# A two-block model layer on one core: index dots between the parts of the value products, gate weights split ahead of Silu, the output product's last chunks by row tile, squares by halves

## The reference

```
h = rmsnorm_2(x, norm_g[l]);  proj = h @ w_in[l]
q, k, v, ga, iq, ik, iw, xr, gr, ma, mb = split(proj)      # rope on q, k, iq, ik
dots  = einsum('bqhd,bsd->bqhs', iq, ik)                   # 16 index heads of 64
score = einsum('bqh,bqhs->bqs', iw, relu(dots));  sel = top_k(score, 64)
attn  = attention over the selected keys                   # 8 heads of 128
y_a = (attn * silu(ga)) @ w_out_attn[l]
hr  = rg_lru(causal_depthwise_conv(xr));  y_b = (hr * silu(gr)) @ w_out_rnn[l]
x = x + (sigmoid(ma) * y_a + sigmoid(mb) * y_b) @ w_o[l]
```

## Time and profile before

| | us |
|---|---|
| median of 3 runs | 1961.88 |
| lowest and highest run | 1961.56, 1962.95 |
| profiled execution, its own time | 1964.03 |
| its span, first to last instruction | 1962.3 |
| second block, first transposes to the end | 1190.3 to 1962.3 |

### The profile page before, as it was taken

How to read it: one execution, slowest core, us unless ns; L and a number is a source line. 1 busy time by engine, 2 the same in 40 slices (tenths; PEclk the granted TensorE clock), 3 DMA queues, 4 the chain that set the end, 5 groups by cost and what they waited for, 6 DMA issues and landing times.

```text
span 1962.3 us, 28235 instructions
## 1 busy us (share of the span) xinstructions
PE 1865.8 (95%) x11294; PEld 1267.1 (65%) x11294; DVE 835.5 (43%) x1885; ACT 671.0 (34%) x1277; POOL 268.9 (14%) x239
## 2 busy tenths in 40 slices
PE   8999999999998999999999999999999999999997
PEld 7784444434447774444444446878889868798996
DVE  4763212211215762111211215556665654756665
ACT  4532111111114531111111113456555444574653
POOL 1400000000000400000000004771000067600000
PEclk9999999999999999999999999999999999999999
DMA  8468999999995469999999995452335744442353
GB/s 290 176 267 372 417 428 426 429 429 428 428 420 193 179 272 389 414 427 427 429 429 429 428 419 201 150 191 87 127 102 180 258 150 161 169 146 89 122 175 114
DMA packets 121431, 557.58 MB, mean 284 GB/s; under 512 B 5009, under 2 KB 49585, under 8 KB 96241
## 3 DMA queue, kind: packets, MB, share of 16 engines
q1 hardware_dynamic: 119696, 551.51, 70.7%
q10 hardware_dynamic: 1440, 4.36, 0.6%
q0 software_dynamic: 192, 0.30, 0.1%
HBM read 555.11 MB, written 1.05 MB: 283 GB/s over the span
## 4 chain that ended last, share of the span: by engine, by line
PE 57%; DVE 4%; DMA 3%; ACT 3%; issue 2%; POOL 0%; SPq 0%; POOLq 0%; DVEq 0%; ACTq 0%
PE bank L2251 7%; PE bank L2282 5%; PE bank L2400 3%; PE bank L2402 3%; PE bank L2401 3%; PE bank L2379 3%; DMA ring<-w_up_dram 3%; PE bank L2380 3%; PE bank L2381 3%; PE bank L2253 3%; PE bank L1974 3%; PE bank L2458 3%; PE bank L2349 2%; PE bank L1983 2%; PE bank L1966 2%
## 5 line engine op out<-in xcount | busy, mean ns | idle before, releaser
L2251 PE MATMUL bank<-ring,work 128*64 128x512 f32 x544 | 240.8, 597 | 10.9 <-issue 10.9
L1622 DVE TENSOR_TENSOR work<-work,bank 64x512 f32<-64x512 f32 x64 | 43.9, 686 | 439.1 <-ACT work L995 439.1
L2253 PE MATMUL bank<-ring,work 128*64 128x512 f32 x512 | 228.9, 602 | 0.0
L811 POOL TENSOR_TENSOR w_lo<-ring,w_hi 128x512 fp32r<-128x512 f32 (+1 forms) x160 | 208.3, 1321 | 77.7 <-ACT w_hi L1040 74.8
L771 POOL TENSOR_TENSOR stat<-stat,power 128x1 f32<-128x1 f32 (+1 forms) x18 | 10.8, 600 | 1506.0 <-DVE stat L1202 1436.6
L995 ACT ACTIVATE work<-bank 64x512 f32<-64x512 f32 x64 | 37.9, 592 | 465.5 <-PE bank L2253 465.5
L1040 ACT CAST w_hi<-ring 128x512 fp32r<-128x512 f32 (+1 forms) x208 | 123.3, 606 | 131.0 <-PE bank L2402 87.1
L2282 PE MATMUL bank<-ring,work 128*64 128x512 f32 x480 | 155.8, 595 | 1.8 <-ACT work L1000 0.4
L2251 PEld LDWEIGHTS bank<-ring,work 128*64 128x64 f32 x544 | 72.7, 138 | 121.7 <-issue 119.8
L1843 DVE TENSOR_TENSOR w_lo<-ring,w_hi 128x512 fp32r<-128x512 f32 (+1 forms) x176 | 115.7, 678 | 79.7 <-ACT w_hi L1153 79.4
L1638 DVE SCALAR_TENSOR_TENSOR act_hi<-bank,stat,act_hi 128x512 fp32r<-128x512 f32 x64 | 48.1, 751 | 211.1 <-ACT act_hi L1005 211.1
(11 more groups left out here) (346 smaller groups left out, 4509.3 us busy)
## 6 DMA issues: line engine op xcount, KB each, us to landing
ring<-w_in_dram SPq DMA_DIRECT2D x34, 2048.0 KB, 9.0
ring<-w_gate_dram SPq DMA_DIRECT2D x34, 2048.0 KB, 20.8
ring<-w_up_dram SPq DMA_DIRECT2D x32, 2048.0 KB, 26.2
ring<-w_down_dram SPq DMA_DIRECT2D x30, 2048.0 KB, 25.8
ring_tail<-w_down_dram SPq DMA_DIRECT2D x18, 2048.0 KB, 23.6
work<-w_gate_dram SPq DMA_DIRECT2D x16, 2048.0 KB, 21.0
work<-w_up_dram SPq DMA_DIRECT2D x16, 2048.0 KB, 26.2
ring_tail<-w_up_dram SPq DMA_DIRECT2D x16, 2048.0 KB, 27.1
```

Source lines behind the costliest of these rows:

```text
L811: pool.tensor_tensor(w_lo[:, g % CHUNKS, 0:n], w[:, k], w_hi[:, g % CHUNKS, 0:n], ALU.subtract).then_inc(chunk_lo, 1)
L2251: pe.matmul(m_bank(m)[gate, :], lhs, wg[:, k], start=(k == 0), stop=(k == KD - 1), skip_group_check=True)
L2253: mu = pe.matmul(m_bank(m)[up, :], lhs, wu[:, k], start=(k == 0), stop=(k == KD - 1), skip_group_check=True)
```

## The change

It leaves the arithmetic and moves work. The dots run in four places between the halves of the two value products, and their PSUM tiles move in the list. The second and third gate pieces' casts and subtractions stand ahead of the Silus, the product with the root and parts of the scan. The first pair's four chunks are made inside attention heads 2 to 4, the hidden state's high and low parts in three pieces from head 5 on, and pair 1's first chunk between the two Silus of the attention gate. The last four chunks of QO + 1 go through row tile 0 first and then row tile 1. Each row's squares are summed in two halves, the first while QO + 1 runs. A layer's first product starts after the first copy and is parted by the second tile's transposes, and six matmuls of zeros stand between the layers. The diff, cut to its core:

Shared names and orders:

```diff
+IDLE_LAYER = 6
...
-        names += [("dots", layer, j) for j in range(12)]
+        names += [("dots", layer, j) for j in range(6)]
         names += [("v", layer, j) for j in range(2, 4)]
+        names += [("dots", layer, j) for j in range(6, 12)]
...
+BY_CHUNK = [(k, t) for k in range(KD) for t in range(NT)]
+ROWS_LAST = BY_CHUNK[0:NT * CHUNKS] + [(k, t) for t in range(NT) for k in range(CHUNKS, KD)]
```

ScalarE:

```diff
+def square_rest(layer, t):
+    emptied(act, ("out2", layer, 2 + t))
+    S(act.activation(h[:, t, 512:], x[:, t, 512:], ACT.Square, accum_out=stat[:, t:t + 1]), sumsq_ready)
...
+            square(stage, t)
         else:
-            emptied(act, ("out2", layer - 1, 2 + t))
-        square(stage, t)
+            square_rest(layer - 1, t)
...
+    def relu_dots(*js):
...
+    relu_dots(0, 1)
...
-    for j in range(12):
-        name = ("dots", layer, j)
-        full(act, name)
-        act.activation(bank(name)[:], bank(name)[:], ACT.Relu).then_inc(relu_ready, 1)
+    relu_dots(2, 3, 4, 5)
     round_weights(QV + 1, CHUNKS, KD)
+    relu_dots(6, 7, 8, 9)
...
+    relu_dots(10, 11)
...
-    for q in (QGR, QGR + 1):
-        if q > QGR:
-            round_weights(q + 1, 0, CHUNKS)
-        for j in range(4 * (q - QGR), 4 * (q - QGR) + 4):
-            silu_gates(j)
-        round_weights(q + 1, CHUNKS, KD)
+    round_weights(QGR + 1, CHUNKS, KD)
+    for j in range(4):
+        silu_gates(j)
+    round_weights(QGR + 2, 0, CHUNKS)
+    for j in range(4, 8):
+        silu_gates(j)
+    round_weights(QGR + 2, CHUNKS, KD)
...
+    def round_hidden(part):
+        act.wait_ge(rnn_gated, RT * (layer + 1))
+        dst, src = ((ui_hi_rest[:], ui[:, KD:]), (act_hi[:, 0:CHUNKS], ui[:, 0:CHUNKS]),
+                    (act_hi[:, CHUNKS:], ui[:, CHUNKS:KD]))[part]
+        act.copy(dst, src).then_inc(ui_hi_ready, 1)
...
+        if 2 <= hh < 4:
+            round_words(QPAIR, 2 * (hh - 2), 2 * (hh - 2) + 2)
+        elif hh >= 5:
+            round_hidden(hh - 5)
...
-    round_words(QPAIR)
-    act.wait_ge(rnn_gated, RT * (layer + 1))
-    act.copy(act_hi[:], ui[:, 0:KD]).then_inc(ui_hi_ready, 1)
-    act.copy(ui_hi_rest[:], ui[:, KD:]).then_inc(ui_hi_ready, 1)
...
+        if half == 1:
+            round_words(QPAIR + 2, 0, 1)
...
-        round_words(QPAIR + 2 * pair + 2, 0, CHUNKS)
+        round_words(QPAIR + 2 * pair + 2, 1 if pair == 0 else 0, CHUNKS)
...
-            round_words(QO + 1)
+            round_words(QO + 1, 0, CHUNKS)
+            for t in range(NT):
+                emptied(act, ("out2", layer, t))
+                S(act.activation(h[:, t, 0:512], x[:, t, 0:512], ACT.Square, accum_out=stat[:, 8 + t:9 + t]),
+                  sumsq_ready)
+            round_words(QO + 1, CHUNKS)
 for t in range(NT):
-    emptied(act, ("out2", DEPTH - 1, 2 + t))
-    square(FINAL, t)
+    square_rest(DEPTH - 1, t)
```

VectorE:

```diff
-    rest_of_weights(QGR + 1, 0, CHUNKS)
+    rest_of_weights(QGR + 1, 0, KD)
...
-    rest_of_weights(QGR + 1, CHUNKS, KD)
+    rest_of_weights(QGR + 2, 0, CHUNKS)
...
-        if j == RT // 2:
-            rest_of_weights(QGR + 2, 0, CHUNKS)
+        if j == 3:
+            rest_of_weights(QGR + 2, CHUNKS, CHUNKS + 2)
+        elif j == 5:
+            rest_of_weights(QGR + 2, CHUNKS + 2, KD)
...
-    rest_of_weights(QGR + 2, CHUNKS, KD)
...
-    S.settle()
-    for j in range(3):
-        gated_hidden(j)
...
+    def rest_of_hidden(part):
+        ks, hi = ((slice(KD, RT), ui_hi_rest[:]), (slice(0, CHUNKS), act_hi[:, 0:CHUNKS]),
+                  (slice(CHUNKS, KD), act_hi[:, CHUNKS:]))[part]
+        dve.wait_ge(ui_hi_ready, 3 * layer + part + 1)
+        dve.tensor_tensor(ui_lo[:, ks], ui[:, ks], hi, ALU.subtract).then_inc(ui_lo_ready, 1)
+    S.settle()
+    for j in range(3):
+        gated_hidden(j)
...
-        else:
-            rest_of_words(QPAIR)
+        if 3 <= hh < 5:
+            rest_of_words(QPAIR, 2 * (hh - 3), 2 * (hh - 3) + 2)
         attended(hh)
-    for part, (ks, hi) in enumerate(((slice(0, KD), act_hi[:]), (slice(KD, RT), ui_hi_rest[:]))):
-        dve.wait_ge(ui_hi_ready, 2 * layer + part + 1)
-        dve.tensor_tensor(ui_lo[:, ks], ui[:, ks], hi, ALU.subtract).then_inc(ui_lo_ready, 1)
+        if hh >= 6:
+            rest_of_hidden(hh - 6)
+    rest_of_hidden(2)
...
+        if half == 1:
+            rest_of_words(QPAIR + 2, 0, 1)
...
-        rest_of_words(QPAIR + 2 * pair + 2, 0, CHUNKS)
+        rest_of_words(QPAIR + 2 * pair + 2, 1 if pair == 0 else 0, CHUNKS)
...
-            rest_of_words(QO + 1)
-    for i in range(4):
+            rest_of_words(QO + 1, 0, CHUNKS)
+    def add_out(i):
...
-        if pc == 1:
-            S.settle()
-            normalise(stage + 1, t)
+    def mean_of_halves(t):
+        dve.wait_ge(sumsq_ready, NT * (stage + 1) + NT * layer + NT + t + 1)
+        dve.scalar_tensor_tensor(out=stat[:, 2 + t:3 + t], in0=stat[:, t:t + 1], scalar=1.0 / D,
+                                 in1=stat[:, 8 + t:9 + t], op0=ALU.mult, op1=ALU.add).then_inc(mean_ready, 1)
+    for t in range(NT):
+        add_out(t)
+    rest_of_words(QO + 1, CHUNKS)
+    dve.wait_ge(sumsq_ready, NT * (stage + 1) + NT * layer + NT)
+    S(dve.tensor_scalar(stat[:, 8:10], stat[:, 8:10], 1.0 / D, EPS, ALU.mult, ALU.add))
+    add_out(2)
+    S.settle()
+    mean_of_halves(0)
+    if layer + 1 == DEPTH:
+        add_out(3)
+        S.settle()
+    root_known(stage + 1, 0)
+    scale_rows(stage + 1, 0)
+    if layer + 1 < DEPTH:
+        add_out(3)
+        S.settle()
+    mean_of_halves(1)
+    root_known(stage + 1, 1)
+    scale_rows(stage + 1, 1)
```

TensorE:

```diff
-    for j in (2 * t, 2 * t + 1):
-        emptied(pe, ("hT", stage, j))
+    if stage < SECOND:
+        for j in (2 * t, 2 * t + 1):
+            emptied(pe, ("hT", stage, j))
...
-    def split_product(q, ready=None, x_hi=hT_hi, x_lo=hT_lo):
+    def split_product(q, ready=None, x_hi=hT_hi, x_lo=hT_lo, order=BY_CHUNK):
...
-        for name in names:
-            claim(name)
-        for k in range(KD):
+        if order[0][0] == 0:
+            for name in names:
+                claim(name)
+        for k, t in order:
...
-            for t in range(NT):
...
+            dst, ts = bank(names[t])[:], slice(t * P, (t + 1) * P)
...
+            if k == KD - 1:
+                done(mm, names[t])
+            elif t == NT - 1:
...
-    w = arrive2(pe, layer, PROPE)
-    for t in range(NT):
-        turn_h(SECOND + layer, t, IDLE_BETWEEN if layer == 0 and t == 0 else 0)
-        by_token(("rope", layer, t), w, 512, t)
+    def first_product(t, k0, k1):
+        name, w = ("rope", layer, t), arrive2(pe, layer, PROPE)
+        if k0 == 0:
+            claim(name)
+        for k in range(k0, k1):
+            if k % 4 == 0:
+                emptied(pe, ("hT", SECOND + layer, 2 * t + k // 4))
+            mm = pe.matmul(bank(name)[:], hT[:, k, t * P:(t + 1) * P], w[:, k], start=(k == 0), stop=(k == KD - 1))
+        if k1 == KD:
+            done(mm, name)
+    if layer == 0:
+        keep_clock(("hT", SECOND, next(j for j in range(4) if TILE[("hT", SECOND, j)] % BANKS >= MOE_BANKS)),
+                   IDLE_BETWEEN)
+    else:
+        keep_clock(("hT", SECOND + layer, 0), IDLE_LAYER)
+    turn_h(SECOND + layer, 0)
+    first_product(0, 0, 6)
+    turn_h(SECOND + layer, 1)
+    first_product(0, 6, KD)
+    first_product(1, 0, KD)
...
-    split_product(QV)
-    for c in range(8, 14):
-        emptied(pe, ("ropeT", layer, c))
-    for j in range(0, 12, 2):
+    def indexer_dots(j):
...
-    split_product(QV + 1)
+    first_chunks, last_chunks = BY_CHUNK[0:NT * CHUNKS], BY_CHUNK[NT * CHUNKS:]
+    split_product(QV, order=first_chunks)
+    for c in range(8, 14):
+        emptied(pe, ("ropeT", layer, c))
+    indexer_dots(0)
+    split_product(QV, order=last_chunks)
+    indexer_dots(2)
+    indexer_dots(4)
+    split_product(QV + 1, order=first_chunks)
+    indexer_dots(6)
+    indexer_dots(8)
+    split_product(QV + 1, order=last_chunks)
+    indexer_dots(10)
...
-        split_pair(pair, ui_hi, ui_lo, (ui_lo_ready, 2 * layer + 2))
+        split_pair(pair, ui_hi, ui_lo, (ui_lo_ready, 3 * layer + 3))
...
-    split_product(QO + 1, merged_lo, act_hi, merged_lo_t)
+    split_product(QO + 1, merged_lo, act_hi, merged_lo_t, ROWS_LAST)
```

28 lines of the change are left out of this document (14 added, 14 removed).

## The result

The changed kernel takes 1935.88 us (median of 4 runs, 1933.22 to 1938.37) against 1962.41 us of the kernel before beside it (4 runs, 1961.56 to 1965.86): ratio 0.9854, 95% interval 0.984 to 0.9869. That is 26.5 us less; 27.0 were forecast, and 1934.9 us as the time. Beside the experiments further down one execution of the kernel before took 7490.19 us where its others took about 1965; it is left out.

The account below looks back on a forecast made before the run. TensorE, busy 95% of the span, was taken as the bound, so only its waits and low clock could yield time. Terms 13.0 + 2.3 + 2.1 + 1.4 + 4.9 + 3.3 = 27.0 us gave median 1934.9 us, range 1928.5 to 1945.

Parts of the forecast that it names:

- 1. Dots: Value products and dots: splitting the dots removes TensorE's stops and the low clock; 6.9 and 6.1 us, 13.0 us together.
- 2. Gates: Gate pieces: weights made ahead of Silu free TensorE 3.1 us earlier, partly lost at attention's first head; 2.3 us.
- 3. Words and hidden state: Attention's end and pairs: making them inside attention removes waits but brings 0.45 and 0.8 us new ones; 2.1 us.
- 4. Start of the layer: Layer 0's start: TensorE no longer waits for both copies of turned rows; 1.4 us.
- 5. Between the layers: Layer boundary: 2.2 us less idle, 1.5 us from the clock not falling, 1.2 us from copies; 4.9 us.
- 6. End: Kernel's end: tile 0's square and root run under TensorE, last scaling ends earlier; 3.3 us.
- A: Rival: new waits longer, gates and hidden-word parts give nothing, drains cost 2 us more; 1941.3 us, chance 0.22.
- B: Rival: no new wait appears, gates give 3.1 and hidden words 2.3 us a layer; 1928.5 us, chance 0.10.
- C: Rival at the dots: clock falls all the same and one 1.7 us wait stays; 10 us less, 1945, chance 0.06.
- D: Rival at the dots: small 64-row dots bring the clock down and value parts don't restore it; 1984 us, chance 0.02.

Follow-up runs that it names:

- d1: Changed kernel with dots 0 to 7 in one go behind the first value product, two amid the second, two behind it: 1937.33 us, ratio 0.9859.
- u1: Changed kernel with all index dots in one go between the two value products again: 1944.81 us, ratio 0.9896 to the kernel before.
- u2: Changed kernel with the gate weights' casts and subtractions behind Silu, product and scans again: 1943.21 us, ratio 0.9898 to the kernel before.
- u3: Changed kernel with pair words and hidden state (still three pieces) split behind attention again: 1935.56 us, ratio 0.9857 to the kernel before.
- u4: Changed kernel with TensorE waiting for both copies of turned rows, first product unparted per row tile: 1937.82 us, ratio 0.986 to the kernel before.
- u5: Changed kernel without the six matmuls of zeros between the layers: 1935.4 us, ratio 0.9851 to the kernel before.
- u6: Changed kernel with the output product's last four chunks by chunk, not by row tile: 1936.37 us, ratio 0.9853 to the kernel before.
- u7: Changed kernel with each row squared whole after its last addition: 1934.89 us, ratio 0.985 to the kernel before.
- b1: Changed kernel with a gate chunk earlier, three scans inside head 0, hidden casts and gated rounding later: 1928.67 us, ratio 0.9823; again 1932.08 us, 0.9824.

## Why the prediction was right

**1. Dots, 13.0 forecast, 12.9 measured** (6.86 and 6.05). No wait for VectorE, the clock at 1.00, as said. Two errors of the sum nearly cancelled: the tile changes took 1.6 us a layer where 1.2 were given to them, and the dots by themselves 5.2, not 5.4. The rows above give both. From the group's first dot to the next value matmul are 1.09 us for 16 instructions of 128 columns and 1.96 us for these and 8 of 256, so 8 of 256 columns have 0.87 us. The 16 of 256 take 1.93 us, twice that and 0.2 more. From 1312.16 to the next group at 1317.83 are 5.67 us, of which 24 value matmuls of 0.2275 us have 5.46, so 0.2 more go there. That is 0.4 us a group, 0.2 a change; four groups have 1.6 us, and 28.64 less this and less 21.84 for 96 value matmuls leaves 5.2 for the dots. d1, with one group fewer, saved 0.5 us. The Trainium skill (TensorEngine Tiling (Array Packing), Key Properties) has TensorE drained at each change of the tiling mode. The trace agrees that a change costs something, and the prediction's estimate of a whole drain, 0.17 us, was near the 0.2 measured. Taking the part away again showed 11.2 us, as the clock's fall was half as long in one layer: the size of this part lies between 11 and 13 us, by how long the clock stays at the lower level.

**2. Gates, 2.3 forecast, 3.5 measured** (1.75 a layer). The term was mis-sized in what attention takes back. TensorE leaves the gate pieces 3.38 us sooner (3.1 said). The prediction let it have 1.1 us of that at the first head. Counted from the recurrent gates' first matmul, VectorE starts its product over the hidden state 3.2 us later, as said. But its scans end only 2.6 us later, not 3.2, and the first logits start 2.1 us sooner, not 1.4: in VectorE's timeline of the changed kernel the last six scans

```profile
1390.83 3.59 DVE L1821 TENSOR_TENSOR_SCAN work<-work 128x256 f32<-128x256 f32 x6
...
1395.47 0.55 DVE L1837 SCALAR_TENSOR_TENSOR work<-bank,work 128x384 f32<-128x384 f32 x1
```

are followed by three gated products and the logits without idle time. And the kernel before had 0.55 us between VectorE's last scaling and the transposes that was TensorE's own. ScalarE's table load ahead of the exponentials takes 0.4 of it back (0.3 said), so head 0 comes 2.3 us sooner. The 0.55 goes again at head 1, which waits as well (5.80 us for 5.25), where the prediction had a wait at head 0 alone:

```profile
1399.19 0.30 PE L2581 MATMUL bank<-ident,work 128*128 128x128 f32 x1 [0.81 <-DVE work L1853]
...
1405.00 0.30 PE L2581 MATMUL bank<-ident,work 128*128 128x128 f32 x1 [0.52 <-DVE work L1853]
```

3.38 - 0.98 - 0.55, less 0.1 us of a longer first part, is 1.75. u1 has that 0.1 us back (26.58 us), so it belongs to the dots, whose part is then 12.7 us and this one 3.7. Undoing the part in u2 gave 1.83 in the layer without the clock's fall, and showed what the prediction had left out: such a stop can cost 1.5 us of clock besides.

**3. Words and hidden state, 2.1 forecast, 2.1 measured** (0.47 and 0.58 a layer). The waits of 0.64, 0.54 and 1.23 us went; the last head's copy is 0.24 us later and not 0.45, the wait ahead of pair 1's second half is 0.94 and not 0.8, and 0.14 us stands ahead of one of pair 1's chunks. The term was right. u3 gives back 0.6 a layer and keeps the three pieces, to which the other 0.45 belongs: the 0.54 us wait was VectorE's wait for the long cast, and went with that, not with the words' earlier place.

**4. Start of the layer, 1.4 forecast, 0.95 measured, and 1.52 by u4.** Of the two waits for copies (0.77 and 0.83 us in u4) one of 0.33 us is left. The table's difference is smaller for a reason outside this part: the products of xr take either 30.65 or 31.16 us in profiles of the same code, in layer 0 the first in the profile of before and the second in that of after. Up to xr's first matmul the stretch fell from 83.02 to 81.55 us: 1.47 us, against the 1.4 forecast.

**5. Between the layers, 4.9 forecast, 5.4 measured**: 2.33 in the gap (2.2 said), 3.05 from the transposes on (1.5 of clock and 1.2 of copies said; u4 has the copies at 1.5). The zeros were said to be part of it; u5 shows that they are not: without them the clock stays and 0.2 us is won. The order by row tiles is the part that carries it, 1.87 us by u6; the halves of squares bring 0.2 us, not 0.4, by u7, as the zeros hide the rest.

**6. End, 3.3 forecast, 3.3 measured** (32.94 to 29.62); 1.0 of it is the order of the rows (u6), none the halves of the squares by themselves (u7). The other 2.3 us no run undid. In the traces row tile 1's addition stood behind row tile 0's scaling before (1955.13 us) and stands ahead of it now (1929.51, the scaling at 1930.24); that this is the 2.3 us is argued, not shown.

**Sum**: 12.9 + 3.5 + 2.1 + 0.95 + 5.4 + 3.3 = 28.15 us, the 28.2 of the second block. Against 27.0 the forecast was 1.2 us short in part 2, 0.5 short in part 5, and by the table 0.45 long in part 4 and 0.1 in part 1. The medians' 26.5 us is less; the first block's length moves by more than this difference between executions, so that the median came within 0.5 us of the forecast is in part luck.

**The rivals.** A (new waits longer, drains 2 us more) fell: parts 2 and 3 gave 3.5 and 2.1 us, not nothing, and the tile changes cost 0.8 us more over both layers, not 2. B (no new wait) fell as a description of the change, which has 2.7, 1.6 and 1.6 us of new or longer waits over both layers; taken as a price it was near, for b1, which cuts these 5.9 us of waits to 2.5, has a second block 5.2 us shorter where B said 6.4. C and D fell: no stop was left among the dots, and dots among full-width products leave the clock at 1.00.

## To carry to other kernels

When a producer of PSUM tiles outruns its reader, spread its groups between other work so that each group fits in the banks that are free. When work is put ahead on an engine's list, ask what stood behind it there, since part of the time comes back at the next chain: of the 3.4 us won at the gates 1.5 came back at the first two heads, and u1 shows these waits unchanged with the dots back in one place. Price a fall of the clock apart from the stop that brings it, and as a range. Before a tile is moved in a list that goes round the banks, write down the bank and the last reader of every tile behind it, up to where the count closes again: two tiles put in brought stops of 8.2 to 8.6 us a layer here, where 1.5 us were to be won.

## What was not expected of the hardware

- The same two stops (1.71 and 2.09 us, 8 instructions between) brought a low clock of 6.8 us three times, twice in before and once in u1, and of 3.41 us once, in u1's layer 1.
- A stop of 2.17 us over the beat in the gate pieces brought 3.41 us of low clock in one of four cases (u2, layer 0; not in layer 1, and in neither layer of before). Single stops of 0.95, 1.7 (d1, both layers) and 1.71 us (u6) brought none; the single stop of 3.51 us between before's layers brought 3.4 us. Stops of 8.2 and 8.6 us brought 6.8 us once and 10.2 us three times, and the clock fell 2.7 to 5.5 us behind the start of the last matmul. The Trainium skill (TensorE: Matmul & The Clock Gate, Part 1: The HAM clock gate) says that the monitor behind the clock runs freely, not in step with the kernel; that the same stops met it at different moments would fit this scatter, but no run here set that moment, so it stays open.
- In the low windows behind the long stops TensorE is busy for 3.85 to 4.44 us only; the rest of the low time falls into the stop and costs nothing.
- The first block, the same code in all profiles, took 1187.5 to 1195.9 us, more than any single part of this change but the dots.
